# A feed-forward's down projection by one level of Strassen's product, in a RetNet and MLA decoder step

## What is computed

```
u = jax.nn.relu(rms_norm(h, norm_ffn) @ w_up)      # 1024 -> 4096
return h + ((u * u) @ w_down).astype(h.dtype)      # 4096 -> 1024
```

## Time and profile before

| what | value |
|---|---|
| median of 3 runs | 1373.8 us (1371.41 to 1376.09) |
| the profiled execution, first to last instruction (its span) | 1370.9 us |
| PE busy | 1348.6 us, 98% of the span |
| DVE, ACT, POOL busy | 758.2, 611.7, 277.4 us |
| the two up and two down stages | from 999.2 us to 1366.1 us |

### The profile page before, as it was taken

The page is one execution under the profiler, slowest core; times in us unless marked ns, Lnnn a source line. Parts: engine busy times, 40 slices in busy tenths (PEclk is TensorE's granted clock), DMA queues, the critical chain, the costliest instruction groups (busy, mean ns, idle before and its releaser), DMA issues.

```text
span 1370.9 us, 31598 instructions
## 1 busy us (share of the span) xinstructions
PE 1348.6 (98%) x11139; PEld 1286.7 (94%) x11139; DVE 758.2 (55%) x1477; ACT 611.7 (45%) x1505; POOL 277.4 (20%) x469
## 2 busy tenths in 40 slices
PE   7999999999999999999999999999999999999998
PEld 7878888999998999999988889899999999999998
DVE  5775555456746657557465656555654533344443
ACT  5643343465655656556534555422233311233211
POOL 0510000355545545555400000000410000000000
PEclk9999999999999999999999999999999999999999
DMA  6033221565646556556454544333232222222232
GB/s 245 20 110 116 72 71 56 181 175 159 186 139 182 161 152 185 158 167 181 128 175 162 208 168 161 111 117 117 91 101 90 94 96 91 82 90 93 94 114 84
DMA packets 110333, 177.59 MB, mean 130 GB/s; under 512 B 13185, under 2 KB 84162, under 8 KB 108482
## 3 DMA queue, kind: packets, MB, share of 16 engines
q1 hardware_dynamic: 110210, 176.05, 40.4%
HBM read 163.98 MB, written 11.89 MB: 128 GB/s over the span
## 4 chain that ended last, share of the span: by engine, by line
PE 86%; issue 2%; SPq 1%; DVE 1%; ACT 0%; DMA 0%; POOL 0%; ACTq 0%; POOLq 0%; DVEq 0%
PE ps L1669 35%; PE ps L1382 25%; PE ps L1843 10%; PE ps L659 5%; PE ps L1408 2%; PE ps L725 1%; PE ps L745 1%; PE ps L1894 1%; PE ps L1883 1%; PE ps L1398 1%; SPq L1001 1%; PE ps L735 1%; PE ps L1897 1%; SPq L997 1%; PE ps L1390 0%
## 5 line engine op out<-in xcount | busy, mean ns | idle before, releaser
L1382 PE MATMUL ps<-wq_hi,ct_hi 128*128 128x260 f32 x1024 | 301.4, 294 | 1.4 <-POOL ct_lo L1064 1.4
L1382 PE MATMUL ps<-wq_hi,ct_lo 128*128 128x260 f32 x1024 | 289.5, 283 | 0.0
L1382 PE MATMUL ps<-wq_lo,ct_hi 128*128 128x260 f32 x1024 | 289.3, 283 | 0.0
L1229 DVE TENSOR_REDUCE k_sums<-k_squares 128x8 f32<-128x512 f32 (+1 forms) x256 | 175.2, 684 | 174.2 <-ACT k_squares L1127 171.7
L1064 POOL TENSOR_TENSOR ct_lo<-ct_raw,ct_hi 128x256 fp32r<-128x256 f32 x256 | 188.9, 738 | 357.5 <-ACT ct_hi L1120 197.4
L1127 ACT ACTIVATE k_squares<-ps 128x512 f32<-128x512 f32 x256 | 153.2, 598 | 169.6 <-PE ps L1382 165.5
L1382 PEld LDWEIGHTS ps<-wq_hi,ct_hi 128*128 128x128 f32 x1024 | 193.2, 189 | 4.9 <-issue 3.8
L1382 PEld LDWEIGHTS ps<-wq_lo,ct_hi 128*128 128x128 f32 x1024 | 193.2, 189 | 0.0
L1382 PEld LDWEIGHTS ps<-wq_hi,ct_lo 128*128 128x128 f32 x1024 | 192.6, 188 | 0.0
L1564 ACT ACTIVATE ring_hi<-ring_raw 128x1024 fp32r<-128x1024 f32 x88 | 89.1, 1013 | 164.7 <-PE ps L1669 122.3
L1569 DVE TENSOR_TENSOR ring_lo<-ring_raw,ring_hi 128x1024 fp32r<-128x1024 f32 x88 | 110.4, 1254 | 25.0 <-ACT ring_hi L1564 23.6
(11 more groups left out here) (329 smaller groups left out, 2906.3 us busy)
## 6 DMA issues: line engine op xcount, KB each, us to landing
ct_raw<-in_ct SPq DMA_DIRECT2D x256, 144.0 KB, 2.4
c_values<-in_c SPq DMA_DIRECT2D x256, 128.0 KB, 2.4
ring_raw<-in_wmain SPq DMA_DIRECT2D x40, 512.0 KB, 3.8
ring_raw<-in_up SPq DMA_DIRECT2D x32, 512.0 KB, 3.2
ring_raw<-in_down SPq DMA_DIRECT2D x32, 512.0 KB, 3.4
z_scratch<-z_staged SPq DMA_DIRECT2D x16, 268.0 KB, 4.2
z<-z_scratch SPq DMA_DIRECT2D x4, 1072.0 KB, 7.0
state_new<-in_state SPq DMA_DIRECT2D x4, 1024.0 KB, 4.9
```

The source lines that it names most:

```text
L1229: dve.tensor_reduce(to, k2[:, j].rearrange("p b h d -> p (b h) d"), AX.X, ALU.add).then_inc(red_done, 1)
L1382: mm = nc.tensor.matmul(k_ps[j % 2][:, f, 0:WQN], ch[:, j, r * P:(r + 1) * P], of_sequence(w, b)[:, r, f, :], start=(r == 0 and x == 0), s ...
```

## The change

The feed-forward becomes a class of its own, `FeedForward`, which runs after the chain and is written out without loops. Its 4096 hidden channels are taken in 4 chunks (`CHUNKS`) of 1024, each with 8 up tiles and 4 steps down (`STEPS_DOWN`). A step makes two output tiles a and b for both halves of the tokens: as a product of 2x2 blocks, with the tiles of u of even and of odd number as the inner index. In the Winograd form of Strassen's algorithm 7 products (`UNITS`), of 12 matmuls each, take the place of 8.

- **Sums of weights.** POOL makes the four sums of a step (`gpsimd`, 512 values of a partition each), from two loaded tiles to `self.sums`. Of the seven left operands four are these sums and three are loaded halves of tiles.
- **Sums of u.** For each pair of up tiles DVE makes four sums (`t`, 260 values each), which ACT and DVE split as the rest: `take_tile(c, 7)`, for instance, is DVE's work on a chunk's last up tile.
- **Sums of products.** Three of the four sums that Winograd's form wants lie in PSUM, where a unit's matmuls add to the bank of an earlier one (`start=False`). After each unit DVE adds the bank to the output (`add`). A unit that goes on with a bank waits until that sum has been taken (`self.added`): P6 for P1's, P7 for P6's, P3 for P5's, P4 for P7's, and the order is P1, P2, P6, P5, P7, P3, P4.
- **The output.** It is summed into h itself (`x_again`), which POOL first multiplies by the mean square (8 instructions over 520 values, after `mean_done`; these come ahead of its first sums of weights). At the end one product with the reciprocal (`finish`) gives y. `y_sum` is gone.
- **The ring.** Four slots in place of two. A unit uses half of a slot. An event's operand is split by ACT and DVE once the product that used the place before has been made, 8 half slots earlier (`BEFORE`, `REFILLED`). So what `take_tile(c, 7)` is followed by on DVE are two splits, P4's operand of the first step and P1's of the second, and then the `add` of P1.
- **Order.** On each engine the order is that of the events: up tiles 0 to 7, then the 28 units; after an event the splits that it released. The mean square is made on PE after up tile 3 of the first chunk, its addition on DVE after `take_tile(0, 3)`, and the reciprocal after `take_tile(0, 4)`.

The core of the diff; the calls of `self.last` in `GatedRetention`, the allocations, the index arithmetic and the stores are left out:

```diff
         self.after.gpsimd(pool)
+        self.last.gpsimd(pool)
...
-    m.acc, oth = p("y_sum", [P, KD, T]), p("o_mla_hi", [P, KD // 2, T], F32R)
+    p.at += 4 * KD * T
+    oth = p("o_mla_hi", [P, KD // 2, T], F32R)
...
-def feed_forward(nc, m, ps, ring):
...
-        def down_dve(dve, i, s, chunk=chunk):
-            t = 2 * i + s
-            dve.wait_ge(ring.product, ring.base + 2 * i + s + 1)
-            if chunk == 0 and s == 0:
-                nc.vector.tensor_copy(twoh(of(m.acc, i)), ps[s][:, :, 0:HF]).then_inc(ring.emptied, 1)
...
             else:
-                dve.wait_ge(ring.emptied, ring.emptied_base + 2 * i + s)
-                nc.vector.tensor_tensor(twoh(of(m.acc, i)), ps[s][:, :, 0:HF], twoh(of(m.acc, i)), ALU.add).then_inc(ring.emptied, 1)
-            if chunk == 1 and s == 1:
-                dve.wait_ge(ring.emptied, ring.emptied_base + 2 * i + 2)
-                if isinstance(i, int) and i == 0:
-                    dve.wait_ge(inv_done, 1)
-                nc.vector.tensor_tensor(of(m.acc, i), of(m.acc, i), mid(real(m.rx)), ALU.mult).then_inc(scaled, 1)
-                dve.wait_ge(scaled, i + 1)
-                nc.vector.tensor_tensor(of(m.acc, i), of(m.acc, i), of(m.h, i), ALU.add).then_inc(y_done, 1)
...
+P1, P2, P6, P5, P7, P3, P4 = range(UNITS)
+B11, B21, B22, T1, T2, T3, T4 = range(UNITS)
...
+    return used, before
+SLOT, BEFORE = _slots()
+REFILLED = [[n for n in range(4, EVENTS) if BEFORE[n] == e] for e in range(EVENTS)]
...
+    def source(self, e):
+        c, j, d, x = place(e)
+        if j is not None:
+            return self.raw[j % 4][:]
+        if x in self.sums:
+            return self.sums[x][:]
+        a, b = (self.raw[n][:].rearrange("p (k two) n -> p two k n", two=2) for n in (2 * d % 4, 2 * d % 4 + 1))
+        return {P1: a[:, 0], P2: a[:, 1], P4: b[:, 1]}[x]
...
+    def sync(self, sp):
+        m = self.m
+        for r in range(2, 16 * CHUNKS):
+            c, n = divmod(r, 16)
+            if r >= 4:
+                c0, n0 = divmod(r - 4, 16)
+                if n0 < UP_TILES:
+                    self.split(sp, PER_CHUNK * c0 + n0)
+                else:
+                    d = (n0 - UP_TILES) // 2
+                    self.split(sp, PER_CHUNK * c0 + UP_TILES + UNITS * d + (P4 if n0 % 2 else P2))
+                    sp.wait_ge(self.summed, self.sums_at(c0, d, P7 if n0 % 2 else P3))
+            src = m.d_up[UP_TILES * c + n] if n < UP_TILES else m.d_down[c // 2][c % 2][n - UP_TILES]
+            sp.dma_start(self.raw[r % 4][:], src).then_inc(self.loaded[r % 4], 16)
...
+    def split_hi(self, act, e):
+        c, j, d, x = place(e)
+        if j is not None:
+            act.wait_ge(self.loaded[j % 4], self.loads(16 * c + j))
+        elif x in self.sums:
+            act.wait_ge(self.summed, self.sums_at(c, d, x))
+        else:
+            r = 16 * c + UP_TILES + 2 * d + (x == P4)
+            act.wait_ge(self.loaded[r % 4], self.loads(r))
+        if BEFORE[e] >= 0:
+            self.made(act, BEFORE[e])
+        self.nc.scalar.activation(self.slot(self.hi, e), self.source(e), ACT.Copy).then_inc(self.ring.hi_done, 1)
+    def split_lo(self, dve, e):
+        dve.wait_ge(self.ring.hi_done, self.ring.base + e + 1)
+        self.nc.vector.tensor_tensor(self.slot(self.lo, e), self.source(e), self.slot(self.hi, e).bitcast(F32), ALU.subtract).then_inc(self.ring.lo_done, 1)
...
+    def scalar(self, act):
+        nc, ps = self.nc, self.ps
+        self.split_hi(act, 2)
+        self.split_hi(act, 3)
+        for e in range(EVENTS):
+            c, j, d, x = place(e)
+            if j is not None:
+                s, i = j % 2, j // 2
+                self.made(act, e)
+                wait(act, self.u_lo, 4 * (4 * c + i))
+                nc.scalar.activation(self.rl[s][:], ps[s][:, :, 0:HF], ACT.Relu).then_inc(self.relu, 1)
+                act.wait_ge(self.relu, UP_TILES * c + j + 1)
+                if s == 0:
+                    nc.scalar.activation(self.uh[:, B11, i, :], self.rl[0][:, 0, :], ACT.Square).then_inc(self.u_hi, 1)
+                else:
+                    nc.scalar.activation(self.uh[:, B21:B22 + 1, i, :], self.rl[1][:], ACT.Square).then_inc(self.u_hi, 1)
+                    for n in range(2):
+                        act.wait_ge(self.u_step, 6 * (4 * c + i) + 4 + 2 * n)
+                        nc.scalar.activation(self.uh[:, T1 + 2 * n:T3 + 2 * n, i, :], self.t[:, 2 * n:2 * n + 2, :], ACT.Copy).then_inc(self.u_hi, 1)
+            for n in REFILLED[e]:
+                self.split_hi(act, n)
...
+        def take_tile(c, j):
+            s, i = j % 2, j // 2
+            pair = 4 * c + i
+            dve.wait_ge(self.relu, UP_TILES * c + j + 1)
+            if s == 0:
+                wait(dve, self.u_step, 6 * pair)
+                wait(dve, self.u_lo, 4 * pair)
+                tt(self.sq[0][:], self.rl[0][:], self.rl[0][:], ALU.mult).then_inc(self.u_step, 1)
+                dve.wait_ge(self.u_step, 6 * pair + 1)
+                dve.wait_ge(self.u_hi, 4 * pair + 1)
+                tt(self.ul[:, B11, i, :], self.sq[0][:, 0, :], self.uh[:, B11, i, :].bitcast(F32), ALU.subtract).then_inc(self.u_lo, 1)
+                tt(t[:, 0, :], self.sq[0][:, 1, :], self.sq[0][:, 0, :], ALU.subtract).then_inc(self.u_step, 1)
+                return
+            tt(self.sq[1][:], self.rl[1][:], self.rl[1][:], ALU.mult).then_inc(self.u_step, 1)
+            dve.wait_ge(self.u_step, 6 * pair + 3)
+            dve.wait_ge(self.u_hi, 4 * pair + 2)
+            tt(self.ul[:, B21:B22 + 1, i, :], self.sq[1][:], self.uh[:, B21:B22 + 1, i, :].bitcast(F32), ALU.subtract).then_inc(self.u_lo, 1)
+            tt(t[:, 1, :], self.sq[1][:, 1, :], t[:, 0, :], ALU.subtract).then_inc(self.u_step, 1)
+            tt(t[:, 2, :], self.sq[1][:, 1, :], self.sq[0][:, 1, :], ALU.subtract).then_inc(self.u_step, 1)
+            dve.wait_ge(self.u_step, 6 * pair + 4)
+            tt(t[:, 3, :], self.sq[1][:, 0, :], t[:, 1, :], ALU.subtract).then_inc(self.u_step, 1)
+            for h in range(2):
+                dve.wait_ge(self.u_hi, 4 * pair + 3 + h)
+                tt(self.ul[:, T1 + 2 * h:T3 + 2 * h, i, :], t[:, 2 * h:2 * h + 2, :], self.uh[:, T1 + 2 * h:T3 + 2 * h, i, :].bitcast(F32),
+                   ALU.subtract).then_inc(self.u_lo, 1)
+        def add(c, d, *parts):
+            for n, (x, bank, t, b) in enumerate(parts):
+                now = self.added_at(c, d, x)
+                self.made(dve, PER_CHUNK * c + UP_TILES + UNITS * d + x)
+                wait(dve, self.added, now - 1 if x in (P2, P7) else now - 2)
+                if c == 0 and x == P1:
+                    dve.wait_ge(self.summed, 2 * d + 2)
+                of = self.acc(t, b)
+                tt(of, self.banks(d)[bank], of, ALU.add).then_inc(self.added, 1)
+        def finish(d, n, t, b):
+            dve.wait_ge(self.added, self.added_at(CHUNKS - 1, d, (P2, P7, P3, P4)[n]))
+            tt(self.acc(t, b), self.acc(t, b), m.rx[:, N_META + b * HF:N_META + (b + 1) * HF], ALU.mult).then_inc(self.scaled, 1)
...
+            if e == 3:
+                dve.wait_ge(self.ms_done, 1)
+                nc.vector.tensor_scalar(self.ms[:], ps[3][:, :, 0:HF], 1.0 / D, EPS, ALU.mult, ALU.add).then_inc(self.mean_done, 1)
+            if e == 4:
+                dve.wait_ge(self.mean_done, 1)
+                nc.vector.reciprocal(halves(real(m.rx)), self.ms[:]).then_inc(self.inv_done, 1)
+            for n in REFILLED[e]:
+                self.split_lo(dve, n)
+    def gpsimd(self, pool):
+        nc, m = self.nc, self.m
+        tt = nc.gpsimd.tensor_tensor
+        pool.wait_ge(self.mean_done, 1)
+        for k in range(KD):
+            of = halves(m.h[:, k, N_META:T])
+            tt(of, of, self.ms[:], ALU.mult).then_inc(self.summed, 1)
+        for n in range(CHUNKS * STEPS_DOWN):
+            c, d = divmod(n, STEPS_DOWN)
+            r, last = 16 * c + UP_TILES + 2 * d, PER_CHUNK * (c if d else c - 1) + UP_TILES + UNITS * ((d - 1) % STEPS_DOWN)
+            a, b = (self.raw[x % 4][:].rearrange("p (k two) n -> p two k n", two=2) for x in (r, r + 1))
+            s1, s2, s3, s4 = (self.sums[x][:] for x in (P5, P6, P7, P3))
+            def free(x):
+                if n:
+                    self.split(pool, last + x)
+            pool.wait_ge(self.loaded[(r + 1) % 4], self.loads(r + 1))
+            free(P5)
+            tt(s1, b[:, 0], b[:, 1], ALU.add).then_inc(self.summed, 1)
+            pool.wait_ge(self.loaded[r % 4], self.loads(r))
+            pool.wait_ge(self.summed, self.sums_at(c, d, P5))
+            free(P6)
+            tt(s2, s1, a[:, 0], ALU.subtract).then_inc(self.summed, 1)
+            free(P7)
+            tt(s3, a[:, 0], b[:, 0], ALU.subtract).then_inc(self.summed, 1)
+            pool.wait_ge(self.summed, self.sums_at(c, d, P6))
+            free(P3)
+            tt(s4, a[:, 1], s2, ALU.subtract).then_inc(self.summed, 1)
...
+        def down(e, c, d, x):
```

(24 more changed lines are left out.)

189 lines of the change are left out of this document (131 added, 58 removed).

## The result

The change makes the kernel slower: 1393.8 us, median of 4 runs (1392.0 to 1395.9), where the kernel before took 1373.8 in the same measurement (4 runs). The ratio is 1.0149, 95% interval 1.0132 to 1.0166. The forecast was 1384 us, 0.7% slower. The sign is right and the loss twice as large; it lies beyond the likeliest case's own range (1377 to 1391 us) and inside the range over all. The profiled execution has a span of 1391.8 us, 20.9 more than before.

A forecast was written before the change was run, and what follows sets the result against it. PE, busy 98% of the span, was taken as the bound. Gain 24.2 us against losses of 34.2 made the span 10.0 us longer, 1380.9, forecast 1384 us (0.7% slower); own range 1377 to 1391, over all 1363 to 1401 us.

The forecast's parts named there:

- the likeliest case's own range: Whole kernel: 1377 to 1391 us, from the clock's bounds and a fifth more or less on stalls; chance 0.52.
- the range over all: Whole kernel, from the first rival to the third: 1363 to 1401 us.
- The gain: Down stages: 192 fewer matmuls at 0.119 us, 22.9 us; shorter tail at the end, 1.3 us; together 24.2 us.
- The new wait at each chunk's start: First step's P6 waits for DVE's addition of P1 behind tile 7 and two splits: 3.45 us, 13.8 in four chunks.
- the steps behind it: Steps making later steps' sums: P6 0.25 us late in each, two such steps in four chunks, 2 us.
- DVE and POOL: Feed-forward: DVE instructions with two SBUF inputs and POOL's run one after the other; additions reading PSUM are not held up.
- The first chunk: POOL's 8 products also queue before the first P6: PE stands 13.3 us, 9.9 more than the 3.45 counted.
- The last chunk: Four finish instructions come into each step: P6 late by 1.95 us, twice, 3.4 us more than in the others.
- The clock: Matmuls at 1.2 GHz after stalls: 1.7 us for the first chunk's, 1.3 for the others, 3.0 us in all.
- The one that ended on the other side: Rival: DVE and POOL don't hold each other up here; only 13.8 us of losses stay, 1363.5 us, faster; chance 0.20.
- shorter queue: Rival, first chunk: POOL's products find DVE's waits, so the 9.9 us goes; 1374 us, no change; chance 0.16.
- The third: Rival: PSUM additions wait for POOL, or its sums exceed 1.17 us: 1396 us, 1400 with low clock every chunk; chance 0.12.

The follow-up runs named there:

- adds_first: The changed kernel with DVE's additions of P1, P2 and P6 moved earlier in its queue in each chunk's first step: 1382.5 us, ratio 1.0070.
- pool_no_read: The changed kernel with POOL's 64 sums and 8 products replaced by memsets, which read nothing (y not the layer's): 1370.3 us, ratio 0.9985.
- clock_fill2: The changed kernel with dummy matmuls into an unused bank where PE waits in each chunk's first step: 1387.3 us, ratio 1.0087.
- early_mean: The changed kernel with the mean square after the first up tile, not the fourth, and the reciprocal after the second: 1391.1 us, ratio 1.0133.
- best2: The changed kernel with adds_first, mean square after the first up tile, POOL's products spread, last chunk's finish products put off: 1367.1 us, 0.9961 of the kernel before.

## Why the prediction was right and where it was wrong

**The gain: right.** 192 matmuls are gone at 0.119 us. The tail's gain of 1.3 us was 1.6: before, the span ended 5.1 us after the last matmul's start, and now 3.5.

**The new wait at each chunk's start: right to a tenth, the steps behind it too cheap.** Predicted at P6, 3.45 us and 0.7 us for the square held back by POOL; measured 3.39 us ahead of P6 and 0.51 within P2, and the square at 1.57 for 0.70. adds_first showed that it was the addition's place in the queue. Outside the start the second and third chunk lose 1.5 and 1.7 us, a wait of 0.41 us and small gaps, where the walk had 0.5.

**DVE and POOL: right.** The splits spread upward, the addition stayed at 0.42, and pool_no_read took the whole of it away. The Trainium skill's page SBUF — State Buffer, "Who interferes with whom", also says that a GpSimd instruction that only writes SBUF is left out of the exclusion, and the memset run agrees: 690 ns beside a memset of 526 ns. That an input in PSUM goes free, which the trace of before showed for 32 values alone, holds at 260: 423 ns.

**The first chunk: right in size, wrong in place.** From the end of up tile 3 at 1023.9 (1001.0 + 4 x 5.72) the walk put P6 at +39.8 us, 1063.7; PE took it up at 1063.33. Until then PE had stood 11.3 us for 13.3, and small gaps and slow matmuls make up for the rest. But it came as three waits, at P1, P2 and P6, since u's low parts were late as well as the addition: I had followed only the event that was last. POOL's sums cost more than the 1.17 us I took, 1.29 alone and 1.5 on the mean, and the walk's end held because other terms were too dear: DVE's 4.7 and 5.1 us for tiles 5 and 7, for two, are some 0.2 us more than their parts add up to. That it held to 0.4 us is in part luck.

**The last chunk: right.** Two waits of 1.63 and 2.15 us for 1.95 each.

All stalls and small gaps were forecast at 31.2 us and came to 33.2.

**The clock: the step that failed.** "The stall of 13.3 us will bring this once; those of some 4 us may or may not, bounds 0 and 5.1 us for three. I take 1.7 + 1.3 = 3.0 us." Measured are 10.3 us. Three things were wrong in it. The waits of 3.4 us did bring the clock down each time, in all three chunks, and in one of them for 6.8 us and not 3.4. The first chunk's stall was several waits with a few matmuls between them, so that the clock stayed low for 17.1 us in place of 3.4: what was issued between the waits, and 6 us behind them, ran at the half rate too. And the price was taken from one stretch of a stage of another kind, and it was given narrow bounds though it had the least in the profile behind it. The Trainium skill has a rule that I had not weighed: the page TensorE: Matmul & The Clock Gate, under "HAM oscillation — how this bites in real kernels", tells of a kernel whose regular waits bring the clock down again before each piece of work, so that the price is paid every time. The changed kernel's trace agrees: four chunks, four stretches at 0.50. clock_fill2 shows the size from the other side: 8.8 us less of slow starts with DVE's work unchanged. The likeliest case's own range was too narrow as well: its two bounds, 3.8 us more for the clock and 6.2 for a fifth of the stalls, reach 1394 us end to end, where it stopped at 1391.

**What is left.** The feed-forward started 1.7 us later in the profile of the changed kernel (1001.0 for 999.3), ahead of anything that the change touches. Over the profiles of this study that start lies between 996.8 and 1002.6 us in no order with what was changed, so it is the execution's own. With it the account closes: -22.9 + 33.2 + 10.3 + 1.7 - 1.6 = 20.7 us, and the spans differ by 20.9. The forecast had 10.0 for the span; of the 10.9 us between them 7.3 are the clock, 2.0 the stalls and 1.7 the start, less 0.3 for the tail.

**The rivals.** The one that ended on the other side was refuted by the splits' own rows. The "shorter queue" was refuted by P6 at 1063.33. The third, which gave 1396 to 1400 us, was nearer to the time than the forecast, but its main cause isn't there: the additions don't wait. Its other condition came true in part, POOL's sums at 1.29 us and more for 1.17, and what that cost beyond the forecast is within the 2.0 us by which all stalls exceeded it. Only its rider, the clock low after every chunk's start, was true, and as it hung on that rival it went into the range and not into the sum.

**What is open.** One chunk's 3.4 us wait brings 3.4 us of low clock and the next one's 6.8. The traces of all eleven kernels show a pattern in this. In the nine places where the feed-forward's clock was low for 6.8 us, it had fallen 0.7 us or more before the end of PE's wait (in the third chunk at 1250.0, with PE back at work at 1250.78). In the 17 places with 3.4 us (two more, of 10.2 and 17.1 us, hold several long waits) it fell from 0.3 us before the end of the wait to 1.5 us behind it (in the second chunk at 1157.85, PE at 1157.70). What sets the moment of the fall is open, and so is why pool_no_read's first wait of 3.31 us and early_mean's of 3.18 us brought none.

## What to carry to other kernels

When an edit makes PE's input come from a slower engine, walk the queue of that engine at the one place where PE has no other work, and price every wait there twice: its length, and the matmuls behind it at the low clock. Where two engines share a port, add up both engines' two-input instructions against the idle time in that stretch, and keep the helper's out of the piece of work that PE waits for; the order alone was worth 24 us here (387.3 us from the feed-forward's first matmul to its last in the changed kernel, 363.2 in best2), more than the 22.9 us of arithmetic saved; the clock that it brought back is in the 24 us. An eighth fewer products in the down stages leaves a margin of 1.7% of this kernel, and the sums that it needs must be hidden all but completely for it to show.
